# Indexer projections as three products of split halves, and top-k masks made inside the attention's loop

## The reference, cut to what matters

```
h = rmsnorm(x, norm_mix[l])
p = split_proj(h @ w_in[l])      # a_q a_k a_v a_iq a_ik a_iw  b_*  c_*  d_*
# mixer A, prompt
dots  = einsum('nthe,nse->nths', iq, ik) * IDX_DIM**-0.5
sc    = einsum('nth,nths->nts', iw * IDX_HEADS**-0.5, relu(dots))   # 4 heads
val, idx = top_k(where(key_pos <= tpos, sc, NEG_BIG), 256)
o = attention of 4 query heads over the selected keys, with a relative bias
```

## Time and profile before

| | |
|---|---|
| time, median of 3 runs | 3362.35 us (3356.21 to 3363.71) |
| the profiled execution, its own time | 3352.43 us |
| its span, first to last instruction | 3350.8 us |
| TensorE matmul busy | 3130.8 us (93%) |
| VectorE busy | 1912.5 us (57%) |
| ScalarE busy | 582.2 us (17%) |
| GpSimd busy | 418.9 us (13%) |
| mean granted TensorE clock | 0.958 of 2.4 GHz |

### The profile page before, as it was taken

One profiled execution on the slowest core, in us unless ns is written; L12 is line 12 of the kernel. 1 busy time (PEld: TensorE's weight loads), 2 busy tenths in 40 slices (PEclk: granted clock), 3 DMA queues, 4 the chain that ended last, 5 costly groups with the idle time before them and its releaser, 6 DMA issues.

```text
span 3350.8 us, 55917 instructions
## 1 busy us (share of the span) xinstructions
PE 3130.8 (93%) x21728; PEld 2864.3 (85%) x21728; DVE 1912.5 (57%) x3459; ACT 582.2 (17%) x1067; POOL 418.9 (13%) x594
## 2 busy tenths in 40 slices
PE   7999978898999999999989999589899999999997
PEld 4599975767899999999956999558688999999997
DVE  3699996687543333333427999966966333333335
ACT  3322113143200000000123221132332000000001
POOL 4143400001000000000041533000000000000000
PEclk9999988799999999999999999797999999999998
DMA  8144434232111111111052543332411111111112
GB/s 273 46 138 129 151 133 162 77 121 105 38 48 41 51 35 55 46 44 51 26 159 62 158 131 129 137 146 85 147 70 38 39 51 51 38 51 38 51 45 96
DMA packets 121147, 292.36 MB, mean 87 GB/s; under 512 B 19445, under 2 KB 70790, under 8 KB 116918
## 3 DMA queue, kind: packets, MB, share of 16 engines
q1 hardware_dynamic: 71938, 129.61, 11.2%
q0 software_dynamic: 33088, 102.84, 9.8%
q10 hardware_dynamic: 15844, 56.12, 4.8%
HBM read 242.24 MB, written 50.74 MB: 87 GB/s over the span
## 4 chain that ended last, share of the span: by engine, by line
PE 66%; DVE 27%; issue 3%; ACT 2%; DVEq 1%; DMA 0%; ACTq 0%; SPq 0%; POOL 0%; POOLq 0%
DVE U L1959 15%; PE PS L1242 14%; PE PS L1240 14%; PE PS L1238 14%; PE PS L758 3%; PE PS L1128 2%; PE PS L1264 2%; PE PS L1266 2%; PE PS L1265 2%; PE PS L819 2%; DVE smu L1965 1%; DVE smu L1977 1%; PE PS L839 1%; PE PS L858 1%; PE PS L795 1%
## 5 line engine op out<-in xcount | busy, mean ns | idle before, releaser
L1959 DVE TENSOR_SCALAR_CACHE_REDUCE U<-U,smu 32x2080 bf16<-32x2080 f32 (+6 forms) x462 | 504.7, 1146 | 13.5 <-issue 1.8
L2366 DVE TENSOR_TENSOR U<-PS,U 128x352 f32<-128x352 f32 x132 | 69.1, 523 | 544.9 <-ACT U L1749 544.8
L1242 PE MATMUL PS<-HNHR,WSR 128*128 128x352 f32 x1920 | 346.2, 322 | 0.0
L1240 PE MATMUL PS<-HnR,WHR 128*128 128x352 f32 x1920 | 345.3, 321 | 0.0
L1238 PE MATMUL PS<-HNHR,WHR 128*128 128x352 f32 x1920 | 345.3, 321 | 0.0
L1242 PEld LDWEIGHTS PS<-HNHR,WSR 128*128 128x128 f32 x1920 | 314.4, 188 | 0.0
L1238 PEld LDWEIGHTS PS<-HNHR,WHR 128*128 128x128 f32 x1920 | 313.5, 188 | 0.0
L1240 PEld LDWEIGHTS PS<-HnR,WHR 128*128 128x128 f32 x1920 | 313.5, 188 | 0.0
L507 POOL DMA_DIRECT2D WS<-wjobs x176 | 94.1, 535 | 1723.0 <-PE PS L1242 1472.7
L1749 ACT ACTIVATE U<-PS 128x352 f32<-128x352 f32 x132 | 61.5, 466 | 1347.8 <-PE PS L1242 1347.8
L1871 DVE CAST WHR<-WS 128x1024 fp32r<-128x1024 f32 (+2 forms) x152 | 94.5, 622 | 296.5 <-DMA WS<-wjobs 296.3
(11 more groups left out here) (294 smaller groups left out, 4938.6 us busy)
## 6 DMA issues: line engine op xcount, KB each, us to landing
WS<-wjobs POOLq DMA_DIRECT2D x113, 512.0 KB, 3.9
WS<-wjobs ACTq DMA_DIRECT2D x50, 512.0 KB, 4.5
WS<-wjobs POOLq DMA_DIRECT2D x48, 384.0 KB, 3.4
Hn<-ckT SPq DMA_DIRECT2D x16, 896.0 KB, 8.4
U<-kT_pool SPq DMA_DIRECT2D x160, 64.0 KB, 2.1
xres<-U SPq DMA_DIRECT2D x2, 4224.0 KB, 15.4
U<-xres SPq DMA_DIRECT2D x4, 2112.0 KB, 7.7
U<-v_pool SPq DMA_DIRECT2D x128, 64.0 KB, 2.3
```

Source lines behind the costliest of these rows:

```text
L1240: mm(out, w(k)[0], x(k)[1], start=False, stop=False)
L1242: i = mm(out, w(k)[1], x(k)[0], start=False, stop=k == n - 1)
L1959: ts(U[0:m, JUNK[i]:JUNK[i] + w // 2].bitcast(BF16), s, CANDF[0:m, i:i + 1], None, op, ALU.add, accum_out=into[0:m, i:i + 1])
L2366: tt(out=x, in0=PS[:, 2 * (t % 3) + 1, 0:CW], in1=U[:, SIL + (t % 3) * CW:SIL + (t % 3 + 1) * CW], op=ALU.mult)
```

## The change

- Jobs 0 to 3 are done as three `float32r` products each (high weights by high activations, high by low, low by high). For the first two jobs the loop over chunks is outside the loop over jobs; job 2 and job 3 follow.
- ScalarE splits off the high halves: of the four jobs' weights into `WHR` (`first_weights`), and of the activations as six copies of 4 blocks x 352 columns into `HDHR` and `HNHR` (`first_hi`), each as soon as the norm has written that half. VectorE makes the low halves: of the activations into `HnR` inside `norm_apply`, of the weights into `WSR` (`first_low`; jobs 0 and 1 behind chunks 0 and 1, job 2 behind the norm, job 3 at the head of `score`).
- The eight subtractions of `HnR` leave the scoring loop. `XHR` is copied from the high halves instead of from `Hn`. The clearing of the indexer's query buffer moves behind the projections. SyncE writes out `X` one step earlier.
- The six masks are made in `attend(0)`: `choose(s)` runs on VectorE ahead of unit s, for s = 0 to 5, and raises `sel`; TensorE waits for `sel` ahead of the masked units of the first head pair. Scratch moves from `FLAGS` to `SS`, the mask of tile 2 gets a place of its own (`SEL2`) and is no longer copied. VectorE waits for `as_ot` ahead of the first mask in place of `as_v`.
- As `SS` is now in use until the last mask, SyncE loads the bias tiles of the second head pair behind `ss_done` (the last mask) and no longer behind `as_ot`. ScalarE's `spread_q(1)` moves from ahead of the attention to unit 7.

```diff
-            def project(L, nos):
-                for n in nos:
...
+            def project(L):
+                def split(n, c):
+                    hi, lo = first_weights(n, 1024), WSR[:, n % NSLOT, 0:1024]
+                    for q in range(3):
+                        if c == 0 and q != 1:
+                            pe.wait_ge((wp_hi, wp_hi, wp_lo)[q], SPLIT_NO[n] + 1)
+                        for k in range(KR):
+                            if n == 0 and q < 2 and k % 4 == 0:
+                                pe.wait_ge((nrm_hi, x_lo)[q], 2 * c + k // 4 + 1)
+                            w = (hi, hi, lo)[q][:, k * P:(k + 1) * P]
+                            x = HnR[:, k, part(c)] if q == 1 else first_hi(k)[:, part(c)]
+                            i = mm(PS[:, job_bank(n) + c, 0:CW], w, x, start=q == 0 and k == 0, stop=q == 2 and k == KR - 1)
+                    return i
+                for c in range(NCH):
+                    for n in range(2):
+                        i = split(n, c)
...
+                pe.wait_ge(pj_ev, 4)
+                for c in range(NCH):
+                    i = split(2, c)
...
+                pe.wait_ge(wp_lo, SPLIT_NO[3] + 1)
...
+                for t in range(9):
+                    m = P if t < 8 else NS
+                    for q in range(3):
+                        for k in range(KR):
+                            x = HnR[:, k, t * P:t * P + m] if q == 1 else first_hi(k)[:, t * P:t * P + m]
+                            i = mm(PS[0:m, base + t // 3, (t % 3) * nc_:(t % 3 + 1) * nc_], x, (hi, hi, lo)[q][:, k, :],
+                                   start=q == 0 and k == 0, stop=q == 2 and k == KR - 1)
...
     # attend, TensorE
                     if masked:
+                        if p == 0:
+                            pe.wait_ge(sel, i - 1)
...
     # project, ScalarE
+                for n in range(3):
+                    loaded(act, L, n)
+                    copy(first_weights(n, 1024), slot(n, 1024)).then_inc(wp_hi, 1)
+                for s in range(2 * NCH):
+                    act.wait_ge(nrm_done, s + 1)
...
+                    i.then_inc(nrm_hi, 1)
...
     # norm_apply, VectorE, for each chunk c behind its rows
+                    if split:
+                        for half in range(2):
+                            v.wait_ge(nrm_hi, 2 * c + half + 1)
+                            tt(out=HnR[:, k, t], in0=Hn[:, k, t], in1=hi.bitcast(F32), op=ALU.subtract).then_inc(x_lo, 1)
+                        if c < 2:
+                            first_low(c, L)
...
     # score, VectorE
-                    if h == 0:
-                        v.wait_ge(x_hi, KR)
-                    for k in (2 * h, 2 * h + 1):
-                        tt(out=HnR[:, k, :], in0=Hn[:, k, :], in1=XHR[:, k, :].bitcast(F32), op=ALU.subtract
-                           ).then_inc(x_lo, 1)
...
     # select and attend, VectorE
-                v.wait_ge(as_v, NB)
-                chosen(*blocks[0], 512)
-                chosen(*blocks[1], 512)
-                v.drain()
-                v.tensor_copy(selected(2), first)
-                for i in range(2, 6):
-                    chosen(*blocks[i], 512)
...
+                v.wait_ge(as_ot, 1)
+                def choose(i):
+                    chosen(*blocks[i], SS, 512).then_inc(sel, 1)
+                    v.drain()
...
                 for s in range(NU + 2):
+                    if k == 0 and s < 6:
+                        choose(s)
...
     # SyncE
-                sp.wait_ge(as_ot, 1)
-                bias_tiles(0, 1)
...
                 sp.wait_ge(ss_done, 3)
+                bias_tiles(0, 1)
```

More of the change, by code:

```diff
@@ L385, in build @@
         STEP_OF = {j: i for i, q in enumerate(STEPS_P) for j in q[1]}
-        SPLIT_NO = {j: n for n, j in enumerate(range(J_A + 4, J_OUT))}
+        SPLIT_NO = {j: n for n, j in enumerate(range(J_A, J_OUT))}
         def unit_bank(u):
@@ L404, in build, with first_hi, first_weights @@
             at_ = (KEPT[i][-1] + 1) % 3
+        def first_hi(k):
+            return HDHR[:, k * TT:(k + 1) * TT] if k < 4 else HNHR[:, k, :]
+        def first_weights(n, w):
+            o = 132 + (n * 1024 if n < 3 else 0)
+            return WHR[:, :, :].rearrange("p a n -> p (a n)")[:, o:o + w]
         def job_bank(n):
@@ L743, in norm_sums @@
                        start=True, stop=True).then_inc(done, 1)
-            def project(L, nos):
-                for n in nos:
[L747 to L763, removed]
-                                i = mm(PS[0:m, base + t // 3, (t % 3) * nc_:(t % 3 + 1) * nc_],
-                                       Hn[:, k, t * P:t * P + m], w[:, k, :], start=k == 0, stop=k == KR - 1)
-                    i.then_inc(pj_ps, 1)
@@ L1457, in project @@
                     if n == 1:
-                        act.wait_ge(nrm_done, 2 * NCH)
+                        loaded(act, L, 3)
+                        copy(first_weights(3, 8 * 132), slot(3, 8 * 132)).then_inc(wp_hi, 1)
                         act.wait_ge(x_out, 16)
                         for k in range(KR):
-                            copy(XHR[:, k, :], Hn[:, k, :]).then_inc(x_hi, 1)
+                            copy(XHR[:, k, :], first_hi(k).bitcast(F32)).then_inc(x_hi, 1)
+                        act.drain()
             def high_part(L, i):
@@ L1570, in attend @@
                         copy(HLOG, PSF[:, 0:CW_KEYS]).then_inc(as_l1, 1)
+                    if k == 0 and s == TILES - 1:
+                        spread_q(1)
                     if s < NU:
@@ L1881, in norm_rows_by, with first_low, norm_apply @@
                 i.then_inc(done, 1)
-            def norm_apply(gain, L):
+            def first_low(n, L):
+                w = 1024 if n < 3 else 8 * 132
+                v.wait_ge(wp_hi, SPLIT_NO[n] + 1)
+                tt(out=WSR[:, n, 0:w], in0=slot(n, w), in1=first_weights(n, w).bitcast(F32), op=ALU.subtract
+                   ).then_inc(wp_lo, 1)
+            def norm_apply(gain, L, split=False):
                 for c in range(NCH):
@@ L1985, in thresholds, with chosen @@
                     v.drain()
-                first = U[:, FIRST:FIRST + 192].bitcast(BF16)
-                def chosen(s, m, i, half):
+                def chosen(s, m, i, at, half):
                     n = s.shape[1]
-                    eq = U[0:m, FLAGS:FLAGS + half].bitcast(BF16)[:, 0:n]
-                    cum = U[0:m, FLAGS + half:FLAGS + half + n]
+                    eq = U[0:m, at:at + half].bitcast(BF16)[:, 0:n]
+                    cum = U[0:m, at + half:at + half + n]
                     ts(eq, s, CANDF[0:m, i:i + 1], None, ALU.is_equal)
@@ L2000, in chosen @@
                     v.drain()
-                    to = first if i == 0 else selected(i + 2) if i < 6 else s
+                    to = selected(i + 2) if i < 6 else s
                     return ts(to, s, -1.0, -NEG, ALU.add, ALU.mult)
@@ L2390, in _ @@
                 v.drain()
[L2391 removed]
+                norm_apply(GMIX, L, True)
+                first_low(2, L)
                 v.wait_ge(rest_in, 32)
```

68 lines of the change are left out of this document (42 added, 26 removed).

## The result

The changed kernel takes 3369.8 us (median of 20 executions) against 3353.6 us for the kernel before beside it, where 3341 and a gain of 21 us were forecast. The ratio of the means (3367.4 and 3355.6 us) is 1.0035, 95% interval 1.002 to 1.005; that of the medians would be 1.0048. A second set of ten gave 3364.7 against 3357.8, 1.0022 [1.0000, 1.0045]. The profiled execution's own time is 3362.8 us, 10.3 above that of before.

The account below looks back on a forecast made before the run. No one engine bounds the whole, so each stage was read by itself. Layers of -7.9 and -12.8 us sum to -21: 3352.4 becomes 3331, plus 9.9 gives 3341 us; range 3326 to 3412, the forecast's own 3328 to 3353.

Parts of the forecast that it names:

- part 1: Price of one split product: 158 ns at 352 columns, 67 ns at 132, so job 3 takes 14.5 us.
- part 3: Scoring: low halves leave VectorE, TensorE bounds at 7.23 us a head; 31.1 us, gaining 3.5 and 2.5 us.
- the halt at the scoring's entry: Scoring: the later query-buffer clearing delays the first ReLU some 0.5 us, so TensorE halts 0.9 us at unit 3.
- the sum: Whole kernel: -7.9 us in the first layer and -12.8 in the second, together -21 us.
- the weight-load one: Job 3: weight loads bound it at 21.6 to 25.5 us; total -7 to +1 us, 3355 to 3363; chance 0.20.
- The dear rival: Job 3: split products of 132 columns cost 227 ns, 49.0 us a layer; +48 us, 3410 us; chance 0.25.
- the third rival: Chunk 1 and first attention units: half clock stays, masks gain nothing; -3 us in all, 3359; chance 0.08.
- A denser stage ahead of it may avoid that: Sample's scores after scoring: half clock at their start might be avoided, up to 3.0 and 2.2 us more, not counted.
- First stage: Projections: +2.3 us in the first layer, -3.6 in the second, with a 4.4 us halt and 1.5 us for half clock.
- Masks: Attention's first units: masks laid between units remove VectorE's waits for TensorE, gaining 6.7 us a layer.
- The price's lower bound: Masks in the attention: gain of nothing if TensorE at half clock gets slow enough to be waited for again.
- The level: Whole kernel: median of the runs shown is 9.9 us above the profiled execution, turning 3331 into 3341 us.

Follow-up runs that it names:

- e4: Changed kernel with some job 3 tiles narrower (66 or 32 moving columns, or 64 stationary columns), values partly left out: 3386.7 us in one execution.
- e7: Changed kernel with only job 3's high-by-high products, 72 of 216: ratio 0.996 to the kernel before.
- e15: Changed kernel with ScalarE's ten small copies ahead of scoring spread, one behind each ReLU from the fourth on: ratio 1.0035 to the kernel before.
- e16: Changed kernel with the ten small copies spread behind scoring's ReLUs and seven added products filling the pause ahead of scoring: ratio 0.9990 to the kernel before.
- e21: e16 repeated without further change: ratio 1.0001 to the kernel before.
- e19: e16 with job 0's and job 1's low weight halves made together after the first chunk and `xres` written later: 3341.2 us, 0.9943 of the kernel before.
- e1: Kernel before with only the masks moved into the attention's loop, projections as they were: ratio 0.9975 to the kernel before.
- e2: Changed kernel with the masks put back ahead of the attention, so the projections alone: ratio 1.0048 to the kernel before.
- e20: Kernel before with masks in the attention's loop, ten copies spread, and two added products filling the pause ahead of scoring: ratio 0.9959 to the kernel before.
- e17: Kernel before with masks in the attention's loop and ScalarE's ten small copies spread behind scoring's ReLUs: ratio 0.9987 to the kernel before.
- e8: Changed kernel with one added, unread product behind each of scoring's 24 units: ratio 1.0086 to the kernel before.

## Why the prediction was wrong

Two steps failed: the price of a short product in part 1, and in part 3 the halt at the scoring's entry, priced at its own length.

**Job 3, the step that failed.** "Both nearest rows say about 67 to 70, so I take 67" ns a product. It was 111 to 112, and job 3 22.9 us, not 14.5: 8.4 us a layer more than the sum has, 16.8 in all, most of the 21 forecast. The line through 352 and 256 columns (158, 118 ns) was right as far as it went; it bends where the stream gets shorter than the weight load, at 132 columns 55 ns against 112. The two records of 32 columns were no evidence on loads: they stand behind products of 512 columns, whose streaming can hide them (that is argued from the order of the rows). Of the rivals the weight-load one is this case, with its 7 to 11 us a layer; it had 0.20. Its total, -7 to +1 us, was still too low, since it too left the scoring at 31.1 us. The Trainium skill's rule in "TensorE: Matmul & The Clock Gate", section "LDWEIGHTS (loading the stationary operand)", columns over 1.2, gives 107 ns for 128 columns. `e4` has 111 to 112, so the trace agrees within 5 ns. The dear rival's 227 ns is excluded. Of the price alone: `e7`, with 144 products a layer less (16.1 us at 112 ns), was 22 us faster than the changed kernel beside it, 28 at equal clock (below).

**Scoring.** The 31.1 us are about right where the clock holds: 30.4 in layer 1, with the halt of 0.65 us at the fourth unit that was forecast as 0.9. In part this is luck: a head takes 6.97 us (1789.27 - 1782.30), 0.70 of it waiting for ScalarE, where 7.23 without waits was forecast. The halt that the step priced at its own 0.9 us was its dear part: there or at the pause ahead TensorE can drop to 1.2 GHz, and then the stage takes 37 to 48 us. Neither the sum nor a rival had that: the halts of the third rival were in chunk 1 and in the attention. "A denser stage ahead of it may avoid that" went the other way. Mis-sized by 17.1 us in layer 0.

The executions agree. Each lists its mean granted clock; over those of the kernel before, 0.001 less goes with 2.2 to 2.7 us more. Brought to 0.957 along each kernel's own line, the changed kernel is at 3362 us in both sets, `e15`, `e16` and `e21` at 3361, the kernel before at 3356 to 3358, masks alone at 3353, `e19` at 3345, `e7` at 3333. By this fit the filled pauses changed nothing but the clock, and of the 12 us that the change loses some 5 are work, the rest clock (its mean is 0.955). It is a correlation, uncertain by 1 to 3 us, with few points for some kernels.

**First stage.** Layer 1: -1.4 for -1.8, right, halt of 3.11 us included (4.4 forecast). Layer 0: the start is 2.1 us later than forecast, because ScalarE's transfer issues took 1.4 us each; the 0.7 of the earlier trace rows did not stay. In the kernel before, in `e1` and in `e19`, where SyncE writes `xres` later, the last of them takes 0.64 to 0.69 us, so it is that write ahead of them. The move on SyncE's queue had been followed for who waits for the transfer, not for what it does to other engines' issues. The rest, 1.4 us, lies about the halt (3.98 us, 4.4 forecast), behind which the clock is 0.50 from 50 to 54 us.

**Masks.** The cover was there, as forecast: the waits at units 1 to 5 went, and no bias tile shows among the waits. The size was off: 4.4 us a layer for 6.7 in the kernel before (`e1`), 2.5 in the changed one. The price's lower bound named the main reason: TensorE is at half clock in this stretch. Unit 6 waits 3.3 to 4.3 us for it in every kernel with the masks in the loop, 1.86 in those without: 2.5 us more in the changed kernel (0.50 and 0.53 over the six microseconds ahead), 1.4 and 1.6 more in `e1` (0.72 in them). The rest is small and was not in the sum: in the changed kernel's first layer the first mask starts 332.7 us behind the search's start, 332.1 before, and VectorE idles 0.2 us five times between masks and units and 0.47 once for ScalarE.

**The level.** 9.9 us of the 3341 came from a median of three; in sets of 18 to 35 executions the kernel before has a median of 3357.6 to 3359.6 us, and in the 20 beside the changed kernel 3353.6. The forecast's own range begins at 3328, where its -31 us give 3331.

**What nobody forecast.** Behind unit 8 each layer is 6.5 to 6.8 us shorter. Of it 2.6 us fall between 691 and 709 us and 1.7 between 798 and 803 in the kernel before, where its clock is down and the changed one's is not. It goes with the split projections, but not cleanly: 1122 to 1129 us in layer 0 and 1134 to 1142 in layer 1 in all profiles that have them (`e2`: 3.6 and 0.5 us below the kernel before), 1127 to 1130 and 1141 to 1143 in those that don't. How an earlier stage does this stayed open; no run was made on it. Also open is why a pause brings the fall in one execution and not in another.

## What to carry over

Price a product by the larger of its stream and its weight load: splitting a product in three pays where the moving operand is wide (352 columns: 474 ns for 623), not where it is 132 (three of 111 for 227). In a stage like this scoring, a wait of TensorE of 0.5 to 2 us at the entry was a risk of 7 to 18 us and not of its own length; laying small copies behind the first results and filling what was left helped. An operation that is moved (a memset, a write-back) should be followed to the first thing that it makes late on every engine.

## What was not expected of the hardware

- At half clock a product with 128 stationary columns takes 213 ns, whatever its width (32 or 132 moving columns, `e4`), where it takes 112 at the full clock: the load goes with the granted clock.
- In `e4` the clock fell inside job 3 in both layers, in or right behind the tiles of 66 moving columns (from 93 us in layer 0), with TensorE counted busy all the time. So being busy by the profile did not keep the clock up; it is one run.
- A kernel with the same work can differ by 15 us and more between executions, and the granted clock differs with it: the changed kernel's 20 go from 3349.3 to 3383.7 us, with mean clocks from 0.949 to 0.962.
- Filling a pause with useless products paid: `e16` against `e15` 3356.1 to 3369.4 us on one chip; `e20` against `e17` 0.9959 to 0.9987, with intervals that overlap. Doing so all through the stage (`e8`) did not.
